# Second block: normalising and turning x by token tile instead of by feature tile

## The chip, the cores and the metric

The kernel runs on one core of a Trainium2 chip. The metric is the device time of one execution in microseconds (us), the lower the better. All tensors are float32. A matmul is made from three float32r passes (low half of one operand times high half of the other, the reverse, and high times high), so each operand exists twice in SBUF: rounded to float32r ("hi") and the rest ("lo").

## The reference

Two transformer blocks run on 512 tokens of width 1024, each with two layers. Only the second block is touched. What matters of it:

```python
def rms_norm(x, g):
    y = x * lax.rsqrt(jnp.mean(x * x, axis=-1, keepdims=True) + EPS)
    return y * g

for l in range(DEPTH):                       # DEPTH = 2
    mod = silu(c) @ w_ada[l] + b_ada[l]      # six vectors of 1024
    sh_m, sc_m, gt_m, sh_f, sc_f, gt_f = jnp.split(mod, 6, axis=-1)
    h = rms_norm(x, g_mix[l]) * (1.0 + sc_m[:, None]) + sh_m[:, None]
    z = h @ w_in[l] + b_in[l]
    ...                                      # two attentions, gates
    x = x + gt_m[:, None] * (merged @ w_out[l])
    h2 = rms_norm(x, g_ffn[l]) * (1.0 + sc_f[:, None]) + sh_f[:, None]
    gate, up = jnp.split(h2 @ w_gu[l], 2, axis=-1)
    x = x + gt_f[:, None] * ((silu(gate) * up) @ w_down[l])
```

## The kernel before

The program is a list of named steps (`steps_second`), and each engine walks the same list in the same order and emits its own part of each step. So the list is the order of the work on every engine; an engine that has to wait in one step does nothing of the steps behind it. Engines meet by semaphores: `bank_full` and `bank_free` for the eight PSUM banks, and one for each kind of result. The second block is a hardware loop over the two layers.

x stands in SBUF with tokens on the partitions, as four token tiles of 128 x 1024 (`x_tok`). The products want features on the partitions. So twice in a layer the normalised x is turned into eight feature tiles of 128 x 512 (`x_pair`): once ahead of the first projection (`which` = 0), once ahead of the gate and up products of the feed-forward part (`which` = 1). These are the steps:

- `rms`, tile tt: ScalarE (ACT) squares x_tok[tt] and sums each row (two instructions: ACTIVATE and READ_ACCUMULATOR). With `which` = 1 it waits for step `add`, in which VectorE (DVE) adds the output of the attention part to that tile: two multiplications from PSUM (L2231) and one addition (L2235).
- `rms_scale`: DVE makes the mean of all four tiles at once (L2075, 128x4), GpSimd (POOL) raises it to the power -0.5 (L2032), and DVE scales the four tiles into `xn` (L2078).
- `turn2`, feature tile d: TensorE (PE) transposes that column of the four xn tiles into one bank (L1821); ACT applies scale and bias of the features and writes the value to SBUF, then copies it, rounded, to `x_pair[0]` (both told as L1917); DVE subtracts the two to get `x_pair[1]` and frees the bank (L2239). The eight d use banks 0, 1, 6, 7 in turn.

The first projection's step `rows qa i` reads feature tiles 2i and 2i+1 and waits for those. The first gate product reads one feature tile after the other and waits for each (`ready`). Weights come through a ring of two slots of 2 MB; SyncE issues a slot's next load once PE has begun to use the other slot. Each piece of weights is rounded by ACT (L642) and its rest made by POOL (L651), at most three pieces ahead in the list; the first four pieces of the first projection come right behind the last `turn2`.

Of the kernel before, what the change touches and what calls it, by code (L numbers as in the profile page):

```python
# [33 lines left out]
F32 = mybir.dt.float32  # L34
# [320 lines left out]
def steps_second():  # L355

    out = []

    def add(name, *args, banks=()):
        out.append((name, args, banks))  # L360

    def rows_of(name):
        add("rows_open", name, banks=(4, 5, 6, 7))
        for i in range(4):
            add("rows", name, i)
        for tt in range(TT):
            add("rows_out", name, tt)
    add("params2")
    add("mod_row", 0, banks=(2,))
    for k in range(4):  # L370
        if k < 3:
            add("mod_row", k + 1, banks=(2 + (k + 1) % 2,))
        add("mod_c", k, banks=(4 + k % 2,))
    def turn_all(which):
        add("rms_scale", which, banks=("power",))
        for d in range(DT):
            add("turn2", which, d, banks=((0, 1, 6, 7)[d % 4],))
    for tt in range(TT):
        add("rms", 0, tt)
    turn_all(0)  # L380
    rows_of("qa")
    add("head_norm", "qa", banks=("power",))
    add("rope", "qa")
    for c in range(4):
        add("rows_T", "qa", c, banks=(2 + c % 2,))
    rows_of("qi")
    add("rope", "qi")
    for c in range(4):
        add("rows_T", "qi", c, banks=(2 + c % 2,))
    rows_of("misc")  # L390
    add("head_norm", "ka", banks=("power",))
    add("rope", "misc")
    for c in range(2):
        add("rows_T", "misc", c, banks=(2 + c % 2,))
    add("open_mask")
    for qt in range(1, TT):
        for h in range(HQ):
            add("idx", qt, h, banks=(h % 2,))
        add("top", qt)

        first = 2 + 2 * qt
        for k in (first, first + 1):
            add("mod_row", k, banks=(2 + k % 2,))
        for k in (first, first + 1):
            add("mod_g" if qt == 1 else "mod_c", k, banks=(4 + k % 2,))

    def attend(a):
        add("s_qk", a, 0, banks=(2,))
        for n in range(TT * HQ + 3):
            if n + 1 < TT * HQ:  # L410
                add("s_qk", a, n + 1, banks=(2 + (n + 1) % 2,))
            if n < TT * HQ:
                add("s_soft", a, n)
            if 2 <= n < TT * HQ + 2:
# [12 lines left out]
            if a == 0 and n in (6, 14):  # L427
                add("mod_g", 10 + n // 8, banks=(1,))
    attend(0)
    for name in ("qb", "kb"):  # L430
        rows_of(name)
        add("head_norm", name, banks=("power",))
        for c in range(4):
            add("rows_T", name, c, banks=(2 + c % 2,))
    rows_of("vb")
    attend(1)
    for n in range(2):
        for dt in range(DT):
            if n or dt > 2:
                add("gate", n, dt, banks=(2 + dt % 2,))  # L440
            if n == 0 and dt in (2, 3, 4, 5):
                add("y2_split", dt - 2)
        for dt in range(DT):
            add("branch", n, dt, banks=(4 + dt % 2,))
            if n == 1 and dt:
                add("merge_split", dt - 1)
    add("merge_split", DT - 1)
    for half in range(2):
        add("out_open", half, banks=tuple(range(4 * half, 4 * half + 4)))
        for i in range(4):  # L450
# [12 lines left out]
    return number(with_splits(out, second_pieces(), {12: ("rows_open", "qb")}))  # L463
# [19 lines left out]
def build(nc, stream, x_in, consts, pack1, ln_rows, edge1, pack2, edge2, pos, c_in, out):  # L483
# [174 lines left out]
    def feed_product(pe, feed, p, out_, begin, right, col=0, ready=None):  # L658

        pe.wait_ge(split_lo, p + 1)  # L660
        release = begin(feed.unit(p))
        w = feed.weights(p)
        k = w[0].shape[1]
        for t in range(k):
            if ready:
                ready(t)
# [990 lines left out]
    rel2 = region(13104, HQ)  # L1657
    stage = region(17200, TT)
    stage_sq = region(19248, TT)
    xn = [region(17200, TT, D), region(7184, TT, D)]  # L1660
    prob2 = region(17200, 4)
    prob2T = region(19248, 2)
    y_rows = region(20272, 2)
# [94 lines left out]
    def second_tensor(pe, layer, steps, uses):  # L1758
# [23 lines left out]
        for name, *args in [(s_[0],) + s_[1] for s_ in steps]:  # L1782
# [30 lines left out]
                        ins = mm(bank[b][:, cols_], C("pick"), sums[:, cols_], True, True)  # L1813
                        ins.then_inc((weights_used, bank_full[b])[half], 1)
            elif name == "turn2":
                which, d = args
                take(b, n)
                for tt in range(TT):
                    if d == 0:
                        pe.wait_ge(xn_ready, which * TT + tt + 1)  # L1820
                    ins = nc.tensor.transpose(bank[b][:, tt * P:(tt + 1) * P], xn[which][:, tt, d * P:(d + 1) * P], C("ident"))  # L1821
                ins.then_inc(bank_full[b], 1)
            elif name in ("rows_open", "out_open"):
                for b, n in zip(banks, use):
                    take(b, n)
            elif name == "rows":
                proj, i = args
                if proj == "qa":
                    for d in (2 * i, 2 * i + 1):
                        drained(pe, uses, "turn2", 0, d)  # L1830
                feed_rows(pe, feed2, feed2.at[name, proj, i], i, uses[("rows_open", proj)][0], x_pair, begin)
            elif name == "rows_T":
                proj, c = args
# [72 lines left out]
                feed_rows(pe, feed2, feed2.at[name, half, i], i, uses[("out_open", half)][0], merged2_pair, begin)  # L1906
            elif name == "gu":
                i, part = args
                take(b, n)
                turned = (lambda t: drained(pe, uses, "turn2", 1, t)) if (i, part) == (0, 0) else None  # L1910
                feed_product(pe, feed2, feed2.at[name, i, part], bank[b][:, :], begin, x_pair, ready=turned).then_inc(bank_full[b], 1)
            elif name in ("down_open", "down", "down_last"):
                feed_down(pe, feed2, name, args[0] if args else None, uses, begin)

    def second_scalar(act, layer, steps, uses):
# [3 lines left out]
        for name, *args in [(s_[0],) + s_[1] for s_ in steps]:  # L1919
# [20 lines left out]
                    .then_inc(square_done, 1)  # L1940
                act.wait_ge(square_done, which * TT + tt + 1)
            elif name == "turn2":
                which, d = args
                if d == 0:
                    act.wait_ge(mod_ready, which + 1)
                filled()
                f(x_lo_value[:, d, :], bank[b][:, :], ACT.Identity, bias=mod[:, 16 * which + d:16 * which + d + 1],
                  scale=gain[:, 8 * which + d:8 * which + d + 1]).then_inc(act_step, 1)
                act.wait_ge(act_step, DT * which + d + 1)
                f(x_pair[0][:, d, :], x_lo_value[:, d, :], ACT.Copy).then_inc(turned_hi, 1)  # L1950
# [70 lines left out]
    def second_gpsimd(pool, layer, steps, uses):  # L2021
        width = {"qa": 32, "ka": 4, "qb": 32, "kb": 32}
        for name, *args in [(s_[0],) + s_[1] for s_ in steps]:
# [3 lines left out]
            if "power" not in banks:  # L2027
                continue
            n = use[banks.index("power")]
            cell = power[:, 0:TT if name == "rms_scale" else width[args[0]]]  # L2030
            pool.wait_ge(stats_ready, n + 1)
            nc.gpsimd.tensor_tensor(cell, cell, half_minus.to_broadcast([P, cell.shape[1]]), ALU.pow).then_inc(power_ready, 1)  # L2032

    def second_vector(dve, layer, steps, uses):
# [6 lines left out]
        for name, *args in [(s_[0],) + s_[1] for s_ in steps]:  # L2041
# [24 lines left out]
            elif name == "mod_g":  # L2066
# [5 lines left out]
            elif name == "rms_scale":  # L2072
                which = args[0]
                dve.wait_ge(square_done, (which + 1) * TT)
                V.tensor_scalar(power[:, 0:TT], sq_sum[:, 0:TT], 1.0 / D, EPS2, ALU.mult, ALU.add).then_inc(stats_ready, 1)  # L2075
                dve.wait_ge(power_ready, uses[(name, which)][1][0] + 1)
                for tt in range(TT):
                    V.tensor_scalar(xn[which][:, tt, :], x_tok[:, tt, :], power[:, tt:tt + 1], None, ALU.mult).then_inc(xn_ready, 1)  # L2078
            elif name == "rows_out":
                proj, tt = args  # L2080
                col, width = ROWS[proj]
# [152 lines left out]
                xs = x_tok[:, tt, :]  # L2234
                V.tensor_tensor(xs, xs, add_tmp[which], ALU.add).then_inc(x_added, 1)  # L2235
            elif name == "turn2":
                which, d = args
                dve.wait_ge(turned_hi, DT * which + d + 1)
                V.tensor_tensor(x_pair[1][:, d, :], x_lo_value[:, d, :], x_pair[0][:, d, :].bitcast(F32), ALU.subtract)\  # L2239
                    .then_inc(bank_free[b], 1)  # L2240
# [244 lines left out]
```

## Time and profile before

| | us |
|---|---|
| median of 3 runs (lowest, highest) | 4796.42 (4795.56, 4799.74) |
| the profiled execution: its time | 4796.42 |
| the profiled execution: its span | 4794.6 |
| PE busy in the span | 4067.4 (85%) |
| DVE, ACT, POOL busy | 1383.3, 1421.9, 1423.7 (29%, 30%, 30%) |

PE is busy most of the time, and each of the others less than a third. The second block begins at 2641 us of the span, and its second layer near 3720 us. The stretches around the two normalisations lie at 2690 to 2715 us and 3317 to 3339 us in layer 0, and again at 3761 to 3786 us and 4389 to 4411 us in layer 1, with the same times inside each to about 0.05 us. A row of a timeline gives start, duration, engine, line, operation, output and inputs, shape, and in brackets how long the engine had been idle and what ended that.

### The profile page before, as it was taken

To read this page: it belongs to the slowest core of one execution; us is meant where nothing else is said; L and a number is where in the kernel's file an instruction comes from. 1 tells how busy PE (TensorE), PEld (TensorE's weight loads), DVE (VectorE), ACT (ScalarE), POOL (GpSimd) and SP (SyncE) were. 2 spreads that over 40 slices of the span, in tenths; PEclk is the share of its full clock that TensorE was granted. 3 is DMA by queue.
4 is the path that set the end of the run, shared out by engine and by line. 5 is a ranking of instruction groups with operands and counts; after the bars stand their busy time and mean duration, and the time that the engine had idled before them with its cause. 6 is when DMAs were issued, how large, how long until landed. Compare 5 with 4: busy or idle time off the path is not lost.

```text
span 4794.6 us, 67666 instructions
## 1 busy us (share of the span) xinstructions
PE 4067.4 (85%) x28944; PEld 3202.7 (67%) x28944; DVE 1383.3 (29%) x2684; ACT 1421.9 (30%) x2380; POOL 1423.7 (30%) x605
## 2 busy tenths in 40 slices
PE   2898889999968979898999477799999467899998
PEld 2688568777856866686877245577887345677886
DVE  2444341311134433413112154213111163213111
ACT  1344242222223431522222213233222213333222
POOL 3200224444440012245444201233443201233443
PEclk9899899999988998998999678899999678899999
DMA  2000212222220001122221332111223231111222
GB/s 86 34 3 3 84 46 99 77 97 88 103 79 7 3 38 68 57 93 79 90 103 71 127 125 87 53 70 71 95 99 114 107 141 65 53 71 71 105 88 106
DMA packets 26699, 366.39 MB, mean 76 GB/s; under 512 B 3104, under 2 KB 3104, under 8 KB 4128
## 3 DMA queue, kind: packets, MB, share of 16 engines
q1 hardware_dynamic: 23040, 335.55, 18.9%
q10 hardware_dynamic: 3360, 26.47, 1.5%
q8 instruction: 235, 3.85, 0.3%
q14 instruction: 64, 0.52, 0.0%
HBM read 359.91 MB, written 2.10 MB: 76 GB/s over the span
## 4 chain that ended last, share of the span: by engine, by line
PE 78%; DVE 11%; ACT 3%; POOL 3%; DMA 2%; issue 2%; DVEq 0%; POOLq 0%; ACTq 0%; PEldq 0%; SPq 0%; PEld 0%
PE bank L581 20%; PE bank L582 20%; PE bank L583 20%; PE bank L854 10%; PE bank L1762 4%; DMA ring<-stream 1%; DVE arena L2173 1%; DVE arena L2172 1%; ACT arena L1165 1%; ACT arena L1917 1%; PE bank L1865 1%; DVE arena L1573 1%; POOL small L2032 1%; PE bank L1794 1%; DVE arena L1476 1%
## 5 line engine op out<-in xcount | busy, mean ns | idle before, releaser
L651 POOL TENSOR_TENSOR ring_r<-ring,hi_ring 128x1024 fp32r<-128x1024 f32 (+1 forms) x522 | 1252.5, 2402 | 2901.9 <-ACT hi_ring L642 2901.5
L581 PE MATMUL bank<-xT_r,ring_r 128*128 128x512 f32 x2288 | 913.7, 399 | 52.3 <-POOL ring_r L651 49.2
L582 PE MATMUL bank<-x_lo_r,hi_ring 128*128 128x512 f32 x2288 | 906.2, 396 | 0.0
L583 PE MATMUL bank<-xT_r,hi_ring 128*128 128x512 f32 x2288 | 902.2, 394 | 0.0
L642 ACT ACTIVATE hi_ring<-ring 128x1024 fp32r<-128x1024 f32 (+1 forms) x522 | 543.9, 1046 | 741.1 <-PE bank L583 391.0
L581 PEld LDWEIGHTS bank<-xT_r,ring_r 128*128 128x128 f32 x2288 | 436.3, 191 | 159.5 <-issue 60.9
L583 PEld LDWEIGHTS bank<-xT_r,hi_ring 128*128 128x128 f32 x2288 | 433.9, 190 | 101.4
L582 PEld LDWEIGHTS bank<-x_lo_r,hi_ring 128*128 128x128 f32 x2288 | 435.4, 190 | 96.5 <-issue 2.1
L854 PE MATMUL bank<-arena 64*64 64x64 f32 (+4 forms) x7456 | 395.3, 250 | 78.3 <-DVE arena L1476 29.6
L1165 ACT ACTIVATE arena<-bank 128x512 f32<-128x512 f32 (+1 forms) x422 | 231.0, 549 | 703.3 <-PE bank L583 496.8
L854 PEld LDWEIGHTS bank<-arena 64*64 64x64 f32 (+2 forms) x7456 | 306.1, 140 | 134.4 <-issue 91.0
L581 PE MATMUL bank<-hi_ring,pairs 128*128 128x512 f32 x864 | 344.3, 399 | 7.6 <-DVE pairs L656 7.6
L582 PE MATMUL bank<-ring_r,pairs 128*128 128x512 f32 x864 | 342.3, 396 | 0.0
L583 PE MATMUL bank<-hi_ring,pairs 128*128 128x512 f32 x864 | 341.9, 396 | 0.0
L1917 ACT ACTIVATE arena<-bank 128x512 f32<-128x512 f32 (+3 forms) x288 | 144.1, 506 | 629.4 <-PE bank L583 190.7
L1762 PE MATMUL bank<-arena 128*128 128x64 f32 (+4 forms) x992 | 232.8, 383 | 85.0 <-DVE small L2196 46.5
L1762 PEld LDWEIGHTS bank<-arena 64*128 64x128 f32 (+1 forms) x992 | 143.7, 207 | 124.0 <-ACT arena L1917 55.2
L656 DVE TENSOR_TENSOR pairs<-arena,pairs 128x512 fp32r<-128x512 f32 x108 | 81.3, 762 | 443.9 <-ACT pairs L647 443.9
L581 PEld LDWEIGHTS bank<-hi_ring,pairs 128*128 128x128 f32 x864 | 164.0, 190 | 48.5 <-issue 9.2
L581 PE MATMUL bank<-hi_ring,x_lo_r 128*128 128x512 f32 (+1 forms) x448 | 175.2, 391 | 22.9 <-POOL ring_r L651 22.9
L1165 ACT ACTIVATE arena<-bank,small 128x64 f32<-128x64 f32 (+1 forms) x222 | 108.9, 496 | 278.8 <-PE bank L583 162.6
L583 PEld LDWEIGHTS bank<-hi_ring,pairs 128*128 128x128 f32 x864 | 163.5, 189 | 39.0
(244 smaller groups left out, 4945.0 us busy)
## 6 DMA issues: line engine op xcount, KB each, us to landing
ring<-stream SPq DMA_DIRECT2D x160, 2048.0 KB, 7.7
arena<-pack ACTq DMA_DIRECT2D x2, 2564.0 KB, 10.3
arena<-ln_rows ACTq DMA_DIRECT2D x5, 1024.0 KB, 5.4
arena<-edge ACTq DMA_DIRECT2D x2, 2048.0 KB, 8.0
arena<-edge ACTq DMA_DIRECT2D x2, 1792.0 KB, 6.8
arena<-pack ACTq DMA_DIRECT2D x2, 1200.5 KB, 5.9
x<-x_in ACTq DMA_DIRECT2D x1, 2048.0 KB, 20.6
out<-x ACTq DMA_DIRECT2D x1, 2048.0 KB, 6.6
```

Source lines behind the costliest of these rows:

```text
L581: first = nc.tensor.matmul(out_, left[1], right[0], start=start, stop=False)
L582: nc.tensor.matmul(out_, left[0], right[1], start=False, stop=False)
L583: return first, nc.tensor.matmul(out_, left[0], right[0], start=False, stop=stop)
L642: nc.scalar.activation(feed.hi(n), feed.raw(n), ACT.Copy).then_inc(split_hi, 1)
L651: nc.gpsimd.tensor_tensor(feed.raw(n, ring_r), feed.raw(n), feed.hi(n).bitcast(F32), ALU.subtract).then_inc(split_lo, 1)
L656: nc.vector.tensor_tensor(lo, feed.hid[:, n, :], hi.bitcast(F32), ALU.subtract).then_inc(hid_lo, 1)
L854: return nc.tensor.matmul(out_, lhsT, rhs, start=start, stop=stop)
L1165: return nc.scalar.activation(out_, in_, func, **kw)
L1476: V.tensor_tensor(T1[g % 2], bank[b][:, :].rearrange("p (b t) -> p b t", b=8), mask.unsqueeze(1).to_broadcast([P, 8, CH]), ALU.mult).then_ ...
L1573: V.tensor_tensor_reduce(out=prob[i % 4][:, m, :], in0=bank[banks[m]][:, :], in1=rel[:, h, at_:at_ + S], scale=1.0, scalar=-3.0e38, op0=AL ...
L1762: return nc.tensor.matmul(out_, lhsT, rhs, start=start, stop=stop)
L1917: return nc.scalar.activation(out_, in_, func, **kw)
```

## The change

`rms_scale` and the turning by feature tile go. Each token tile is taken through by itself: `rms` of tile tt now has its own mean, power (128x1) and scaling, and `turn2` of tile tt transposes the eight 128 x 128 squares of that tile into banks 0 and 1, four to a bank. ACT then applies scale and bias with four instructions of 128 x 128 for each bank (each square has its own features), and copies, and DVE subtracts, four squares at once. `xn` has two tiles instead of four, so scaling tile tt waits until tile tt-2 is turned. With `which` = 0 the steps alternate (`rms` 0, `turn2` 0, `rms` 1, ...); with `which` = 1 `turn2` of a tile comes one tile later. The first projection and the first gate product wait for the last token tile. Squares, transposes, scalings, copies and subtractions have the same number of elements in all; the scale-and-bias instructions become 32 instead of 8 in each turning.

```diff
-    def turn_all(which):
-        add("rms_scale", which, banks=("power",))
-        for d in range(DT):
-            add("turn2", which, d, banks=((0, 1, 6, 7)[d % 4],))
     for tt in range(TT):
-        add("rms", 0, tt)
-    turn_all(0)
+        add("rms", 0, tt, banks=("power",))
+        add("turn2", 0, tt, banks=(0, 1))
...
     for tt in range(TT):
         add("add", 0, tt)
-        add("rms", 1, tt)
-    turn_all(1)
+        add("rms", 1, tt, banks=("power",))
+        if tt:
+            add("turn2", 1, tt - 1, banks=(0, 1))
+    add("turn2", 1, 3, banks=(0, 1))
...
# TensorE
+                which, tt = args
+                pe.wait_ge(xn_ready, which * TT + tt + 1)
+                for i in range(2):
+                    take(banks[i], use[i])
+                    for k in range(4):
+                        ins = nc.tensor.transpose(bank[banks[i]][:, k * P:(k + 1) * P], xn[which][:, tt % 2, (4 * i + k) * P:(4 * i + k + 1) * P],
+                                                  C("ident"))
+                    ins.then_inc(bank_full[banks[i]], 1)
...
-                    for d in (2 * i, 2 * i + 1):
-                        drained(pe, uses, "turn2", 0, d)
+                if proj == "qa" and i == 0:
+                    drained(pe, uses, "turn2", 0, TT - 1)
...
+                if i == 0 and part == 0:
+                    drained(pe, uses, "turn2", 1, TT - 1)
...
# ScalarE
+                for i in range(2):
+                    filled(banks[i], use[i])
+                    for k in range(4):
+                        d = 4 * i + k
+                        ins = f(dst[:, d, tt * P:(tt + 1) * P], bank[banks[i]][:, k * P:(k + 1) * P], ACT.Identity,
+                                bias=mod[:, 16 * which + d:16 * which + d + 1], scale=gain[:, 8 * which + d:8 * which + d + 1])
+                    here = slice(4 * i, 4 * i + 4), slice(tt * P, (tt + 1) * P)
+                    ins.then_inc(act_step, 1)
+                    act.wait_ge(act_step, 8 * which + 2 * tt + i + 1)
+                    f(x_pair[0][:, here[0], here[1]], dst[:, here[0], here[1]], ACT.Copy).then_inc(turned_hi, 1)
...
# VectorE
+            elif name == "rms":
+                dve.wait_ge(square_done, which * TT + tt + 1)
+                V.tensor_scalar(power[:, tt:tt + 1], sq_sum[:, tt:tt + 1], 1.0 / D, EPS2, ALU.mult, ALU.add).then_inc(stats_ready, 1)
+                dve.wait_ge(power_ready, n + 1)
+                if tt >= 2:
+                    drained(dve, uses, "turn2", which, tt - 2)
+                V.tensor_scalar(xn[which][:, tt % 2, :], x_tok[:, tt, :], power[:, tt:tt + 1], None, ALU.mult).then_inc(xn_ready, 1)
```

What ScalarE does ahead of the first projection, before. Rows with `x 128x1024` are the squares, `arena<-bank,small` the scale and bias from PSUM, `xT_r<-arena` the rounded copy; a row says what it waits for, and ends with how many follow each other alike.

```order
L1917 ACTIVATE arena,small<-x 128x1024
L1917 ACTIVATE arena,small<-x 128x1024 [waits square_done] x3
L1917 ACTIVATE arena<-bank,small 128x512 [waits bank0_full,mod_ready,square_done]
L1917 ACTIVATE xT_r<-arena 128x512 [waits act_step]
L1917 ACTIVATE arena<-bank,small 128x512 [waits bank1_full]
L1917 ACTIVATE xT_r<-arena 128x512 [waits act_step]
```

The same place now:

```order
L1914 ACTIVATE arena,small<-x 128x1024
L1914 ACTIVATE arena<-bank,small 128x128 [waits bank0_full,mod_ready,square_done]
L1914 ACTIVATE arena<-bank,small 128x128 x3
L1914 ACTIVATE xT_r<-arena 128x4x128 [waits act_step]
L1914 ACTIVATE arena<-bank,small 128x128 [waits bank1_full]
L1914 ACTIVATE arena<-bank,small 128x128 x3
L1914 ACTIVATE xT_r<-arena 128x4x128 [waits act_step]
L1914 ACTIVATE arena,small<-x 128x1024
```

The four squares stood together ahead of everything; now the square of the second tile stands behind the whole turning of the first.

VectorE between the output product and the gate product, before (L2231 and L2235 are step `add`, L2075 the mean, L2078 the scaling into xn, L2239 the subtraction):

```order
L2231 TENSOR_TENSOR arena<-bank,arena 128x512 [waits bank3_full,x_added]
L2231 TENSOR_TENSOR arena<-bank,arena 128x512 [waits bank7_full,bank3_free]
L2235 TENSOR_TENSOR x<-x,arena 128x1024 [waits bank7_free]
L2075 TENSOR_SCALAR small<-small 128x4 [waits square_done]
L2078 TENSOR_SCALAR arena<-x,small 128x1024 [waits power_ready]
L2078 TENSOR_SCALAR arena<-x,small 128x1024 x3
L2239 TENSOR_TENSOR x_lo_r<-arena,xT_r 128x512 [waits turned_hi] x8
```

The third and fourth tile at that place now (L2235, L2239, L2078, L2082 and L2245 are these steps in the changed file):

```order
L2235 TENSOR_TENSOR arena<-bank,arena 128x512 [waits bank2_full,x_added]
L2235 TENSOR_TENSOR arena<-bank,arena 128x512 [waits bank6_full,bank2_free]
L2239 TENSOR_TENSOR x<-x,arena 128x1024 [waits bank6_free]
L2078 TENSOR_SCALAR small<-small 128x1 [waits square_done]
L2082 TENSOR_SCALAR arena<-x,small 128x1024 [waits bank1_free,bank0_free,power_ready]
L2245 TENSOR_TENSOR x_lo_r<-arena,xT_r 128x4x128 [waits turned_hi] x2
L2235 TENSOR_TENSOR arena<-bank,arena 128x512 [waits bank3_full,x_added]
```

The additions of the four tiles stood ahead of the mean; now mean, scaling and the two subtractions of the tile before stand between one tile's addition and the next one's.

## Rows read from the trace of the kernel before

**Rows 1.** The chain that ended last, by engine, from the page.

```profile
PE 78%; DVE 11%; ACT 3%; POOL 3%; DMA 2%; issue 2%; DVEq 0%; POOLq 0%; ACTq 0%; PEldq 0%; SPq 0%; PEld 0%
```

**Rows 2.** Timeline, layer 0, ahead of the first projection: start, duration, engine, what.

```profile
2690.83 1.05 ACT L1917 ACTIVATE arena<-x 128x1024 f32<-128x1024 f32 x1
...
2694.30 0.17 DVE L2064 TENSOR_TENSOR small<-small,arena 128x8 f32<-128x8 f32 x1
2694.36 1.06 ACT L1917 ACTIVATE arena<-x 128x1024 f32<-128x1024 f32 x1
...
2695.55 0.17 DVE L2075 TENSOR_SCALAR small<-small 128x4 f32<-128x4 f32 x1 [1.07 <-ACT arena L1917]
2695.79 1.02 POOL L2032 TENSOR_TENSOR small<-small 128x4 f32<-128x4 f32 x1 [56.70 <-DVE small L2075]
2696.85 2.74 DVE L2078 TENSOR_SCALAR arena<-x,small 128x1024 f32<-128x1024 f32 x4 [1.14 <-POOL small L2032]
...
2697.66 0.47 PE L1821 MATMUL bank<-const,arena 128*128 128x128 f32 x1 [3.87 <-DVE arena L2078]
...
2699.65 3.93 PE L1821 MATMUL bank<-const,arena 128*128 128x128 f32 x17 [0.19 <-DVE arena L2078]
2700.24 0.78 ACT L1917 ACTIVATE arena<-bank,small 128x512 f32<-128x512 f32 x1 [4.73 <-PE bank L1821]
2701.05 0.63 ACT L1917 ACTIVATE xT_r<-arena 128x512 fp32r<-128x512 f32 x1
2701.59 0.76 ACT L1917 ACTIVATE arena<-bank,small 128x512 f32<-128x512 f32 x1
2701.72 0.69 DVE L2239 TENSOR_TENSOR x_lo_r<-arena,xT_r 128x512 fp32r<-128x512 f32 x1 [2.12 <-ACT xT_r L1917]
...
2710.90 3.88 ACT L642 ACTIVATE hi_ring<-ring 128x1024 fp32r<-128x1024 f32 x4
...
2714.60 0.79 PE L581 MATMUL bank<-hi_ring,x_lo_r 128*128 128x512 f32 x1 [7.03 <-POOL ring_r L651]
```

**Rows 3.** Timeline, layer 0, between the output product and the gate product.

```profile
3317.77 1.06 ACT L1917 ACTIVATE arena<-x 128x1024 f32<-128x1024 f32 x1 [3.59 <-DVE x L2235]
3317.77 1.42 DVE L2231 TENSOR_TENSOR arena<-bank,arena 128x512 f32<-128x512 f32 x2
...
3320.55 1.06 ACT L1917 ACTIVATE arena<-x 128x1024 f32<-128x1024 f32 x1 [1.62 <-DVE x L2235]
...
3325.96 1.06 ACT L1917 ACTIVATE arena<-x 128x1024 f32<-128x1024 f32 x1 [1.55 <-DVE x L2235]
...
3328.43 2.74 DVE L2078 TENSOR_SCALAR arena<-x,small 128x1024 f32<-128x1024 f32 x4 [1.12 <-POOL small L2032]
...
3338.80 0.77 PE L581 MATMUL bank<-xT_r,ring_r 128*128 128x512 f32 x1
```

**Rows 4.** Groups by line and form: busy us, mean ns of one, idle before.

```profile
L1150 ACT ACTIVATE xT_r<-bank 128x512 fp32r<-128x512 f32 x40 | 23.5, 597 | 166.1 <-PE bank L1136 166.1
...
L2078 DVE TENSOR_SCALAR arena<-x,small 128x1024 f32<-128x1024 f32 x16 | 11.0, 749 | 4.5 <-POOL small L2032 4.5
```

**Rows 5.** Timeline of ScalarE in the first block: instructions back to back.

```profile
256.14 1.69 ACT L1165 ACTIVATE arena<-bank,small 128x512 f32<-128x512 f32 x3 [2.24 <-PE bank L854]
...
684.82 0.28 ACT L1165 ACTIVATE arena<-bank 128x128 f32<-128x128 f32 x1 [0.30 <-PE bank L854]
685.00 0.19 ACT L1165 ACTIVATION_READ_ACCUMULATOR arena<-bank 128x1 f32 x1
```

**Rows 6.** Timeline of POOL in the first block: a power of 128x1.

```profile
2607.83 0.55 POOL L1337 TENSOR_TENSOR small<-small 128x1 f32<-128x1 f32 x1 [4.47 <-DVE small L1627]
```

**Rows 7.** Busy time by stretch, layer 0: per engine, then PE clock.

```profile
2714.60:2718.90 4.30, 4.30 (x10) 3.43 (x11) 0.00 (x0) 0.18 (x1) 4.30 (x2) 0.50 0.00 0
2718.90:2723.00 4.10, 4.10 (x19) 3.26 (x19) 0.00 (x0) 0.52 (x1) 2.48 (x2) 0.99 0.00 0
3338.80:3340.20 1.40, 1.40 (x5) 1.14 (x4) 0.77 (x2) 1.37 (x3) 0.00 (x0) 0.50 0.00 0
```

**Rows 8.** Timeline of ScalarE in the projections of layer 0.

```profile
2770.33 0.54 ACT L642 ACTIVATE hi_ring<-ring 128x400 fp32r<-128x400 f32 x1 [8.28 <-DMA ring<-stream]
```

More of the change, by code:

```diff
@@ L656, in feed_vector, with feed_product @@
         nc.vector.tensor_tensor(lo, feed.hid[:, n, :], hi.bitcast(F32), ALU.subtract).then_inc(hid_lo, 1)
-    def feed_product(pe, feed, p, out_, begin, right, col=0, ready=None):
+    def feed_product(pe, feed, p, out_, begin, right, col=0):
         pe.wait_ge(split_lo, p + 1)
@@ L664, in feed_product @@
         for t in range(k):
-            if ready:
-                ready(t)
             first, last = pair_product(out_, [a[:, t, col:col + P] for a in w], [a[:, t, :] for a in right],
@@ L1659, in build @@
     stage_sq = region(19248, TT)
-    xn = [region(17200, TT, D), region(7184, TT, D)]
+    xn = [region(17200, 2, D), region(7184, 2, D)]
     prob2 = region(17200, 4)
@@ L1815, in second_tensor @@
             elif name == "turn2":
[L1816 to L1822, printed above, removed]
+                which, tt = args
[6 more added lines that the diff above has]
+                    ins.then_inc(bank_full[banks[i]], 1)
             elif name in ("rows_open", "out_open"):
@@ L1908, in second_tensor @@
                 i, part = args
+                if i == 0 and part == 0:
+                    drained(pe, uses, "turn2", 1, TT - 1)
                 take(b, n)
-                turned = (lambda t: drained(pe, uses, "turn2", 1, t)) if (i, part) == (0, 0) else None
-                feed_product(pe, feed2, feed2.at[name, i, part], bank[b][:, :], begin, x_pair, ready=turned).then_inc(bank_full[b], 1)
+                feed_product(pe, feed2, feed2.at[name, i, part], bank[b][:, :], begin, x_pair).then_inc(bank_full[b], 1)
             elif name in ("down_open", "down", "down_last"):
@@ L1942, in second_scalar @@
             elif name == "turn2":
-                which, d = args
-                if d == 0:
+                which, tt = args
+                if tt == 0:
                     act.wait_ge(mod_ready, which + 1)
[L1946 to L1950, printed above, removed]
+                dst = x_lo_value
+                for i in range(2):
[8 more added lines that the diff above has]
+                    f(x_pair[0][:, here[0], here[1]], dst[:, here[0], here[1]], ACT.Copy).then_inc(turned_hi, 1)
             elif name in ("split", "hid_split"):
@@ L2029, in second_gpsimd @@
             n = use[banks.index("power")]
-            cell = power[:, 0:TT if name == "rms_scale" else width[args[0]]]
+            cell = power[:, args[1]:args[1] + 1] if name == "rms" else power[:, 0:width[args[0]]]
             pool.wait_ge(stats_ready, n + 1)
@@ L2071, in second_vector @@
                 V.tensor_tensor(o, o, bank[b][:, :], ALU.add).then_inc(bank_free[b], 1)
[L2072 to L2078, printed above, removed]
+            elif name == "rms":
+                which, tt = args
+                dve.wait_ge(square_done, which * TT + tt + 1)
[4 more added lines that the diff above has]
+                V.tensor_scalar(xn[which][:, tt % 2, :], x_tok[:, tt, :], power[:, tt:tt + 1], None, ALU.mult).then_inc(xn_ready, 1)
             elif name == "rows_out":
@@ L2236, in second_vector @@
             elif name == "turn2":
[L2237 to L2240, printed above, removed]
+                which, tt = args
+                for i in range(2):
+                    dve.wait_ge(turned_hi, 8 * which + 2 * tt + i + 1)
+                    here = slice(4 * i, 4 * i + 4), slice(tt * P, (tt + 1) * P)
+                    V.tensor_tensor(x_pair[1][:, here[0], here[1]], x_lo_value[:, here[0], here[1]],
+                                    x_pair[0][:, here[0], here[1]].bitcast(F32), ALU.subtract).then_inc(bank_free[banks[i]], 1)
             elif name == "s_turn" and args[0] == 1:
```

1 line of the change is left out of this document (removed).

## The prediction

> **What bounds the kernel now.** I read the chain that ended last first: 78% of it is PE, 11% DVE, 3% each ACT and POOL [rows 1]. So PE sets the time wherever it has work, and a change of other engines' work counts only where PE stands waiting for it. Then I read the two stretches that the change touches, in the timeline, each in layer 0; layer 1 repeats them.
>
> Ahead of the first projection PE is idle for its next product from the modulation vectors on, except for the transposes. What ends last there is a single file: four squares on ACT from 2690.83 us, the mean, the power, the scalings, and then ACT's eight pairs of scale-and-bias and copy, 1.33 us apart, up to 2710.90 us, where ACT turns to the weights. POOL makes their rest and PE begins at 2714.60 us [rows 2]. The end of ACT's turning sets that start; 3.70 us of weight work follow it.
>
> Ahead of the gate product the additions of x come first, one tile every 2.71 to 2.78 us on DVE, the last square at 3325.96 us; the scalings start at 3328.43 us and PE's first gate product at 3338.80 us [rows 3]. From there PE runs on while the last feature tiles are still being turned, because that product takes them one by one. So the number to compare is 3338.80 us with the moment at which the last token tile is ready after the change.
>
> **The change, part by part.** First, the costs of one tile in the new form. The square to the start of the mean is 1.19 us (2694.36 to 2695.55 us), and from a square to ACT's next instruction 1.18 us (the three intervals from 2690.83 to 2694.36 us) [rows 2]. Mean to power is 0.24 us, then the power, then 0.04 us [rows 2]. The power of 128x4 took 1.02 us there; one of 128x1 took 0.55 us [rows 6]. I take 0.55, together 0.83 us; the other end is 1.02. The scaling is 0.75 us [rows 4], and 0.06 us later PE begins (2697.66 after 2696.85 + 0.75 us) [rows 2]. Four transposes into a bank: the seventeen in 3.93 us are 0.22 us apart, and from the last one of a bank to ACT it is 0.59 us (2699.65 to 2700.24 us), so 3 x 0.22 + 0.59 = 1.25 us [rows 2]. These rows are at half clock (0.50), as PE's are whenever it has been idle here [rows 7]. The second bank's transposes hide behind the first bank's ACT work.
>
> The scale-and-bias on 128x128 isn't in the trace. On 128x512 it takes 0.76 us [rows 2]. A plain one takes 0.60 us at 512 columns [rows 4] and 0.28 us at 128 [rows 5], so I size one at 0.76 - 0.32 = 0.44 us. Back to back they overlap. From below: the plain 128x128 is followed by the next instruction after 0.18 us [rows 5]. From above: no overlap at all, 0.44 us. Between: three of 128x512 with a scale operand took 1.69 us, which is 0.50 us apart for 0.69 us each, an overlap of 0.19 us [rows 5]. That is the nearest row in kind of operand, and I take 0.44 - 0.19, about 0.24 us apart. One bank's share is then 3 x 0.24 + 0.44 + 0.03 = 1.19 us to the copy, and 0.54 us from the copy to ACT's next instruction (2701.05 to 2701.59 us) [rows 2]: 1.73 us, for a tile 3.46 us. A copy of four squares costs what one of 512 columns does, as the first block's copy of that shape shows (0.60 us) [rows 4]. From a copy to DVE's subtraction it is 0.67 us, and that takes 0.69 us [rows 2].
>
> The Trainium skill (ScalarE: Activation LUTs, "What ACT_TABLE_LOAD costs") gives an ACTIVATE a fixed part of 186 ns, about 93 ns more for each per-partition operand, and an overlap of only about 93 ns. Its figures put a 128x128 with both operands at some 0.48 us, spaced 0.39 us: an estimate that would add about 11 us to the sum below. The three instructions above came out closer than that rule has them, 0.50 us apart where it gives 0.61, so I stay with the row [rows 5].
>
> First place. What is late now is no longer ACT's copying alone: the order puts square tt+1 behind turning tt on ACT, and its mean behind it on DVE. Nothing of tile tt+1 overlaps with tile tt. Tile 0: DVE is free after the modulation at about 2694.50 us [rows 2], so the mean starts there, the scaling at 2695.33, the transposes at 2696.14, ACT at 2697.39, done at 2700.85 us. Each further tile is the whole ring: 1.19 + 0.83 + 0.75 + 0.06 + 1.25 + 3.46 = 7.54 us, three of them 22.62 us. ACT turns to the weights at 2723.47 instead of 2710.90 us: 12.57 us later, and PE with it. The finer wait of the projection for two feature tiles hid nothing before, since the weights were later anyway; replacing it costs nothing.
>
> Second place. Tile 0 is added as before; its square starts at 3317.77 us [rows 3]. Then DVE waits: mean at 3318.96, scaling from 3319.79 to 3320.54 us. Only now comes the addition of tile 1, which had started at 3317.77 us. An addition up to the next square is 2.78 us (3317.77 to 3320.55 us) [rows 3], so square 1 is at 3323.32, and ACT starts turning tile 0 at 3324.50 us. Its second subtraction ends 1.73 + 1.19 + 0.67 + 0.69 = 4.28 us later, at 3328.78 us, and lets the addition of tile 2 begin. This ring (addition 2.78, square 1.18, turning 4.28) is 8.24 us, and the scaling of the next tile falls into it beside ACT. Two of them bring the end of turning tile 2 to 3345.26 us. For tile 3 the banks are free only now: 0.06 + 1.25 to the last half's ACT work, 1.19 + 0.67 + 0.69 + 0.05 to PE: 3349.17 us against 3338.80, 10.37 us. The gate product had started with all but its last feature tiles ready; that overlap goes, and is inside this number.
>
> Clock. The gate product ran at half clock (1.2 GHz) for its first 1.40 us, having the transposes close ahead of it; the first projection, after 7.03 us of idle PE, for 4.30 us, before it went to 2.4 GHz [rows 2, 7]. After the change the gate product also follows sparse transposes and about 2.5 us of nothing, so I give it 4.30 us: (4.30 - 1.40) / 2 = 1.45 us more. Below: nothing.
>
> The adds that wait have only the steps of this normalisation behind them; no weight load is queued there. SyncE's loads wait for PE's progress and move with it. After both places the work is PE's again, without slack.
>
> Sum: 2 layers x (12.57 + 10.37 + 1.45) = 48.8 us. The profiled execution took 4796.42 us for a span of 4794.6 us, which is also the median, so the forecast is 4845 us, 1.0% slower. Bounds: spacing of 0.18 us takes 0.18 us from each half, of 0.44 adds 0.60; eight halves are on the path at the first place and seven at the second, 30 in all: -5.4 or +18.0 us. The power at 1.02 us counts at each tile at the first place and once at the second: 2 x 5 x 0.47 = +4.7 us. Clock -2.9 us. So 4837 to 4868 us.
>
> **Rivals.** A, the small ACT instructions don't overlap: the upper end, 4845 + 18 = 4863 us. For it: a scale-and-bias is longer than a plain one, and how two such operands overlap no row shows. Against it: the three back to back [rows 5].
>
> B, the tiles do overlap and it gets faster. The mechanism would be at the second place: the additions keep their pace, and only the last tile remains behind the last square at 3325.96 us [rows 3]. Then 1.19 + 0.83 + 0.75 + 0.06 + 1.25 + 1.73 + 1.19 + 0.67 + 0.69 + 0.05 = 8.41 us lead to 3334.37 us, 4.43 us sooner, and spread transposes keep the clock up, 0.70 us more. At the first place ACT alone would be the bound, 2697.39 + 8 x 1.73 = 2711.23 us, 0.33 us later. In all 2 x (4.43 + 0.70 - 0.33) = 9.6 us gained, 4787 us, and 4783 with the tighter spacing. It decides from the point where DVE's addition of tile 1 starts before the scaling of tile 0. Against it: DVE and ACT take the list in order, and the wait stands ahead of the addition.
>
> C, part of the delay is hidden by a transfer that would have been waited for anyway: ACT stood 8.28 us for weights after the second projection had begun [rows 8]. If those came at a fixed time, 2 x 8.3 us would be given back: 4829 us. Against it: that load is issued only when PE takes the slot before it.
>
> D, both places are covered by something I don't see, and the time stays.
>
> **How the numbers follow.** Forecast 0.79, A 0.12, C 0.03, B 0.04, D 0.02. The range of 4828 to 4868 us takes in the forecast's bounds, A and C, with some 1 in 10 outside. What a measurement of this kernel can tell from no change is about 0.2%, 9.6 us. Slower: forecast, A and C, 0.94. B lies at that edge, so faster 0.03 and within 0.2% 0.03.
>
> **What would show it.** Right: at the first place squares on ACT about 7.5 us apart, with ACT and DVE idle in between for PE; at the second place additions about 8.2 us apart where they were 2.7; PE's idle time ahead of the first gate product up by some 10 us; DVE's waits for ACT's copies grown. The spacing of four 128x128 on ACT gives the disputed price directly. Wrong: squares of four tiles close together, a gate product starting less than 25 us after the first square of its place, or a stage between the two places that has become shorter.

## The result, and the profile after

The changed kernel takes 4853.55 us in the median (4852.16 to 4857.79, 4 runs), the kernel before in the same runs 4795.99 us (4792.81 to 4799.74, 4 runs). The ratio is 1.0118 with a 95% interval of 1.0103 to 1.0134: 57.6 us, or 1.2%, slower. Forecast were 48.8 us and 4845 us, with a range of 4828 to 4868 us. Of all executions told below one, of the kernel with the small instructions alone, took 13941 us; it counts in the median of its six and stands outside the ratio.

First the changed kernel's page, busy time by engine and the chain that ended last:

```profile
PE 4068.8 (84%) x28944; PEld 3207.1 (66%) x28944; DVE 1387.2 (29%) x2696; ACT 1445.4 (30%) x2476; POOL 1428.4 (29%) x617
...
PE 77%; DVE 11%; ACT 4%; POOL 3%; issue 3%; DMA 2%; DVEq 0%; POOLq 0%; ACTq 0%; PEldq 0%; SPq 0%; PEld 0%
```

PE does the work that it did (4068.8 us busy against 4067.4), and the span grew by 55.6 us. So most of the time went into waits of PE, and a little into its clock, shown below. ACT is 23.5 us busier, on 96 more instructions; in the chain ACT went from 3% to 4% and "issue" from 2% to 3% [rows 1].

The first place in layer 0, from the end of the modulation to the first weight piece, two tiles of the four, and then PE's first product (timeline: start, duration, engine, what):

```profile
2690.91 0.17 DVE L2067 TENSOR_TENSOR small<-small,arena 128x8 f32<-128x8 f32 x1
2691.00 0.15 DVE L2078 TENSOR_SCALAR small<-small 128x1 f32<-128x1 f32 x1
2691.22 0.55 POOL L2035 TENSOR_TENSOR small<-small 128x1 f32<-128x1 f32 x1 [55.42 <-DVE small L2078]
2691.81 0.75 DVE L2082 TENSOR_SCALAR arena<-x,small 128x1024 f32<-128x1024 f32 x1 [0.66 <-POOL small L2035]
...
2692.62 1.97 PE L1817 MATMUL bank<-const,arena 128*128 128x128 f32 x8 [2.22 <-DVE arena L2082]
2693.85 1.50 ACT L1914 ACTIVATE arena<-bank,small 128x128 f32<-128x128 f32 x4 [5.27 <-PE bank L1817]
2695.39 0.63 ACT L1914 ACTIVATE xT_r<-arena 128x512 fp32r<-128x512 f32 x1
2695.92 1.49 ACT L1914 ACTIVATE arena<-bank,small 128x128 f32<-128x128 f32 x4
...
2697.44 0.63 ACT L1914 ACTIVATE xT_r<-arena 128x512 fp32r<-128x512 f32 x1
2697.98 1.04 ACT L1914 ACTIVATE arena<-x 128x1024 f32<-128x1024 f32 x1
...
2706.11 1.04 ACT L1914 ACTIVATE arena<-x 128x1024 f32<-128x1024 f32 x1
...
2722.38 3.88 ACT L640 ACTIVATE hi_ring<-ring 128x1024 fp32r<-128x1024 f32 x4
...
2726.08 0.79 PE L579 MATMUL bank<-hi_ring,x_lo_r 128*128 128x512 f32 x1 [7.07 <-POOL ring_r L649]
```

This answers to [rows 2]. The square of each next tile (`x 128x1024`) comes right behind the copy of the tile before, and the squares are 8.13 us apart (2697.98, 2706.11 us): the single file. From the end of the modulation to the weights it is now 2722.38 - 2690.91 = 31.47 us, and was 2710.90 - 2694.30 = 16.60 us: 14.87 us more in this layer, where 12.57 were forecast. PE's product begins 3.70 us behind that in both kernels.

The second place in layer 0, ACT's squares and DVE's additions, then PE's first gate product:

```profile
3331.47 1.06 ACT L1914 ACTIVATE arena<-x 128x1024 f32<-128x1024 f32 x1 [3.59 <-DVE x L2239]
...
3332.66 0.15 DVE L2078 TENSOR_SCALAR small<-small 128x1 f32<-128x1 f32 x1 [1.22 <-ACT arena L1914]
3333.48 0.75 DVE L2082 TENSOR_SCALAR arena<-x,small 128x1024 f32<-128x1024 f32 x1 [0.67 <-POOL small L2035]
3334.15 1.41 DVE L2235 TENSOR_TENSOR arena<-bank,arena 128x512 f32<-128x512 f32 x2
...
3342.35 0.69 DVE L2245 TENSOR_TENSOR x_lo_r<-arena,xT_r 128x512 fp32r<-128x512 f32 x1 [1.36 <-ACT xT_r L1914]
3342.96 1.41 DVE L2235 TENSOR_TENSOR arena<-bank,arena 128x512 f32<-128x512 f32 x2
...
3351.70 1.41 DVE L2235 TENSOR_TENSOR arena<-bank,arena 128x512 f32<-128x512 f32 x2
...
3364.89 0.79 PE L579 MATMUL bank<-xT_r,ring_r 128*128 128x512 f32 x1 [3.19 <-issue]
```

The additions (L2235 here) start at 3334.15, 3342.96 and 3351.70 us, 8.8 us apart where they were 2.7 [rows 3], each right behind the scaling or the last subtraction of a tile. From the first square to the gate product it is 33.42 us, before 21.03 us: 12.39 us more, forecast 10.37.

Busy time by stretch of the changed kernel around the start of the gate product (start and end, its length, then busy us and instructions of PE, its weight loads, DVE, ACT and POOL; the number behind POOL's is PE's clock):

```profile
3364.89:3371.00 6.11, 6.11 (x14) 4.78 (x15) 0.00 (x0) 0.03 (x1) 2.37 (x1) 0.50 0.69 244
3371.10:3375.00 3.90, 3.90 (x19) 3.16 (x18) 0.69 (x1) 1.47 (x2) 0.00 (x0) 1.00 0.35 147
```

It runs at half clock (1.2 GHz) for 6.1 us, where it was 1.4 us before and 4.3 us had been forecast [rows 7]. Half of the 4.7 us more is 2.35 us, forecast 1.45. The first projection went the other way. Its product begins at half clock in both kernels, but for a shorter time in the changed one:

```profile
2726.08:2729.20 3.12, 3.12 (x7) 2.48 (x8) 0.00 (x0) 0.18 (x1) 3.12 (x2) 0.50 0.02 5
3827.91:3831.80 3.89, 3.89 (x9) 3.12 (x10) 0.00 (x0) 0.18 (x1) 3.89 (x2) 0.50 0.00 0
```

These are its layers 0 and 1. The kernel before had about 4.4 us in layer 0 and 5.3 us in layer 1, here the latter:

```profile
3785.55:3790.80 5.25, 5.25 (x12) 4.12 (x13) 0.00 (x0) 0.18 (x1) 5.25 (x3) 0.50 0.00 0
```

That is 1.3 us less in each layer now, which gives back 0.65 us a layer. Together 2 x (14.87 + 12.39 + 2.35 - 0.65) = 57.9 us; the medians differ by 57.6 us. The spans of the two profiles differ by 55.6 us only, because the part ahead of the first place, which the change doesn't touch, was 3.4 us shorter in this one (2690.91 against 2694.30 us at the same instruction). In the profiles of the next five kernels that instruction lies between 2688.36 and 2695.54 us, so the span of a single profile tells a change to some us and no better.

### The profile page after: what moved, and what is told of

Same layout as the page of the kernel before. It is cut to its first block, busy times and chain, and to the rows that moved or that the text cites. A ratio compares the mean times of both kernels' runs of the same rounds, so it can differ in the third digit from the quotient of the medians.

```text
span 4850.2 us, 67804 instructions
## 1 busy us (share of the span) xinstructions
PE 4068.8 (84%) x28944; PEld 3207.1 (66%) x28944; DVE 1387.2 (29%) x2696; ACT 1445.4 (30%) x2476; POOL 1428.4 (29%) x617
## 4 chain that ended last, share of the span: by engine, by line
PE 77%; DVE 11%; ACT 4%; POOL 3%; issue 3%; DMA 2%; DVEq 0%; POOLq 0%; ACTq 0%; PEldq 0%; SPq 0%; PEld 0%
PE bank L579 20%; PE bank L580 20%; PE bank L581 19%; PE bank L850 10%; PE bank L1758 4%; ACT arena L1914 2%; DVE arena L2177 1%; DVE arena L2176 1%; ACT arena L1161 1%; PE bank L1861 1%; DMA ring<-stream 1%; DVE arena L1569 1%; POOL small L2035 1%; PE bank L1790 1%; DVE arena L1472 1%
```

## The experiments

Two theories. O: the order of the list puts the tiles in single file, and an engine's wait for one tile holds up its work on the next. P: the price of splitting eight scale-and-bias instructions into thirty-two is what costs, whatever the order. All kernels were timed against the kernel before on the same chip.

**The new form at one place only.** Both kernels hold both forms. The first has the new one ahead of the first projection:

```diff
     for tt in range(TT):
-        add("rms", 0, tt)
-    turn_all(0)
+        add("rms_t", 0, tt, banks=("power",))
+        add("turn_t", 0, tt, banks=(0, 1))
```

> The kernel before with the new form at the first place only (ahead of the first projection); the turning ahead of the gate product stays by feature tile. Theory O (the order of the list puts the tiles in single file, and each place pays by itself): the first place costs what it costs in the changed kernel, 14.9 us a layer from the first square to ACT's first weight piece, and the second nothing: 2 x 14.9 = 30 us, 4826 us. Theory P (the price of the small ScalarE instructions is all of it, the same at both places): 8 halves x 0.74 us = 5.9 us a layer, 4808 us.

Measured: 4826.17 us, ratio 1.0061 (1.0048 to 1.0074). From the first square to the weights it was 34.95 us, 14.88 more than before; the second place took 21.02 us, as before. The second has it ahead of the gate product:

```diff
-        add("rms", 1, tt)
-    turn_all(1)
+        add("rms_t", 1, tt, banks=("power",))
+        if tt:
+            add("turn_t", 1, tt - 1, banks=(0, 1))
+    add("turn_t", 1, 3, banks=(0, 1))
```

> The kernel before with the new form at the second place only (ahead of the gate product). Theory O: 12.4 us a layer until the gate product starts and about 2 us more for its longer stretch at half clock, 2 x 14.5 = 29 us, 4825 us; together with the first place this makes the whole change. Theory P: about 12 us in all, 4808 us.

Measured: 4823.38 us, ratio 1.0057 (1.0045 to 1.0070). PE's first gate product in its timeline:

```profile
3350.06 0.79 PE L583 MATMUL bank<-xT_r,ring_r 128*128 128x512 f32 x1 [3.33 <-DVE x_lo_r L2282]
```

The first square of that place was at 3316.51 us, so this is 33.55 us behind it, as in the changed kernel. The two places cost 30 and 28 us. Together that is 58 us against 57.6, closer than the intervals promise, since each ratio is known to about 6 us. So within that they add up, and neither is given back later. P's numbers for them (12 us each) are far off.

**The small instructions alone.** The kernel before with the scale-and-bias split, everything else as it was:

```diff
-                f(x_lo_value[:, d, :], bank[b][:, :], ACT.Identity, bias=mod[:, 16 * which + d:16 * which + d + 1],
-                  scale=gain[:, 8 * which + d:8 * which + d + 1]).then_inc(act_step, 1)
+                for k in range(4):
+                    ins = f(x_lo_value[:, d, k * P:(k + 1) * P], bank[b][:, k * P:(k + 1) * P], ACT.Identity,
+                            bias=mod[:, 16 * which + d:16 * which + d + 1], scale=gain[:, 8 * which + d:8 * which + d + 1])
+                ins.then_inc(act_step, 1)
```

> The kernel before, turned by feature tile, but with each scale-and-bias of 128x512 done as four of 128x128 (the price of the small instructions alone, with the order as it was). Theory P: this alone gives most of the 57 us of the change. Theory O: a pair of ACT steps grows from 1.33 to 2.07 us, 8 x 0.74 = 5.9 us a layer at the first place; at the second the gate product's last feature tile becomes ready about 4.8 us later than PE wants it; 2 x (5.9 + 4.8) = 21 us, 4817 us.

Measured: 4817.57 us, ratio 1.0043 (1.0030 to 1.0056), 22 us. At the first place, from the first square to the weights, 25.89 us, 5.82 more than before, as O had it. At the second the total was right and its parts not: the gate product began 23.93 us after the first square, 2.9 us later than before, because the transposes wait for banks that ACT empties more slowly; and then it ran at half clock for 5.3 us instead of 1.4:

```profile
3350.05:3355.40 5.35, 5.35 (x15) 4.18 (x14) 2.08 (x3) 5.29 (x14) 0.00 (x0) 0.50 0.67 214
3355.40:3360.00 4.60, 4.60 (x21) 3.49 (x20) 1.38 (x3) 3.75 (x6) 2.23 (x1) 1.00 0.49 210
```

2.9 + 1.9 = 4.8 us; none of it was the expected wait for the last feature tile, since PE ran without a gap from 3350.05 us on. So the price of the small instructions is real, but it is 22 us with the old order, not 57.

**The order.** The changed kernel, all tiles normalised before the first is turned. That needs four xn tiles in place of two, so the wait for tile tt-2 goes too, and the scratch of the squares lies elsewhere (the diff below shows the order only). In the changed kernel's trace the two xn tiles held nothing up at these places: each scaling in layer 0 started 0.66 or 0.67 us after DVE fell idle, and its power (POOL) ended that.

```diff
-        add("rms", 0, tt, banks=("power",))
-        add("turn2", 0, tt, banks=(0, 1))
+        add("rms", 0, tt, banks=("power",))
+    for tt in range(TT):
+        add("turn2", 0, tt, banks=(0, 1))
...
         add("add", 0, tt)
-        add("rms", 1, tt, banks=("power",))
-        if tt:
-            add("turn2", 1, tt - 1, banks=(0, 1))
-    add("turn2", 1, 3, banks=(0, 1))
+    for tt in range(TT):
+        add("rms", 1, tt, banks=("power",))
+    for tt in range(TT):
+        add("turn2", 1, tt, banks=(0, 1))
```

> The changed kernel with its small instructions and turning by token tile, but ordered so that all four tiles are added and normalised before the first is turned (xn has four tiles again, and the scratch of the squares lies elsewhere for that). Theory O: most of the loss goes. First place: ACT turns from 2697.4 us (by the times of the kernel before) for 4 x 4.14 us, 3 us a layer later than before instead of 14.9. Second place: the gate product starts 7.4 us later instead of 12.4, its half clock stays: 2 x (3 + 7.4 + 2) = 25 us, 4821 us. Theory P: no change from the changed kernel, 4853 us.

Measured: 4818.24 us, ratio 1.0048 (1.0035 to 1.0061). ACT at the first place (timeline):

```profile
2684.89 1.05 ACT L1915 ACTIVATE arena<-x 128x1024 f32<-128x1024 f32 x1
...
2700.48 1.51 ACT L1915 ACTIVATE arena<-bank,small 128x128 f32<-128x128 f32 x4
2702.02 0.63 ACT L1915 ACTIVATE xT_r<-arena 128x512 fp32r<-128x512 f32 x1
...
2708.78 3.88 ACT L641 ACTIVATE hi_ring<-ring 128x1024 fp32r<-128x1024 f32 x4
```

23.89 us from the first square to the weights, 3.8 more than before, against 14.9 in the changed kernel. The same small instructions run here with hardly a gap. At the second place the gate product began 29.36 us after the first square (3315.41 to 3344.77 us), 8.3 more than before. The half clock did not stay as expected; it was half as long as in the changed kernel:

```profile
3344.77:3347.90 3.13, 3.13 (x7) 2.47 (x8) 0.00 (x0) 0.03 (x1) 2.37 (x1) 0.50 0.50 99
```

This kernel and the one before it have the same ScalarE instructions in two good orders and cost about the same, 22 and 23 us. Of the change's 57.6 us some 35 therefore go with the order and 22 with the instructions, by these two differences, each known to about 6 us.

**One step moved.** The changed kernel with the next tile's addition ahead of this tile's scaling:

```diff
+    add("add", 0, 0)
     for tt in range(TT):
-        add("add", 0, tt)
+        if tt + 1 < TT:
+            add("add", 0, tt + 1)
         add("rms", 1, tt, banks=("power",))
```

> The changed kernel with one line of the list moved: at the second place the addition of tile tt+1 stands ahead of the mean and scaling of tile tt. The same instructions. Theory O (DVE's wait for square and power stands ahead of the next addition, and ACT's turning behind it): the gate product starts about 7.3 us a layer sooner than in the changed kernel, 4839 us. Rival (the ACT work of the turning is the bound at this place): no change, 4853 us.

Measured: 4837.01 us, ratio 1.0090 (1.0074 to 1.0105). DVE at the second place:

```profile
3328.85 1.42 DVE L2237 TENSOR_TENSOR arena<-bank,arena 128x512 f32<-128x512 f32 x2
3330.30 1.22 DVE L2241 TENSOR_TENSOR x<-x,arena 128x1024 f32<-128x1024 f32 x1
3331.44 0.15 DVE L2080 TENSOR_SCALAR small<-small 128x1 f32<-128x1 f32 x1
3332.26 0.75 DVE L2084 TENSOR_SCALAR arena<-x,small 128x1024 f32<-128x1024 f32 x1 [0.67 <-POOL small L2037]
3332.93 1.41 DVE L2237 TENSOR_TENSOR arena<-bank,arena 128x512 f32<-128x512 f32 x2
```

The mean (L2080) now starts without a wait for its square, which ran beside the addition, and the third addition comes 4.1 us after the second instead of 8.8. The gate product began 25.52 us after the first square, 7.9 us sooner than in the changed kernel. No instruction was added or taken away, so this is the place of the wait in the list, with what follows from it (the half clock behind it was 3.6 us long instead of 6.1).

**A better version, in three steps.** Since the first place is a single file before the change too, its squares, mean, power and scalings can go where the engines idle, ahead of the modulation vectors (the kernel before, turning by feature tile kept):

```diff
     add("params2")
+    for tt in range(TT):
+        add("rms", 0, tt)
+    add("rms_scale", 0, banks=("power",))
     add("mod_row", 0, banks=(2,))
```

> The kernel before with squares, mean, power and scaling of the first place moved ahead of the modulation vectors, where ACT, DVE and POOL are idle and x is ready. Turning by feature tile stays. If those steps are the single file that the rows of before show there, ACT starts turning when the modulation is ready (2694.5 us instead of 2700.24 us): 5.7 us a layer, 11 us in all, 4785 us. Rival (PE's start hangs on the weights, loaded from 2691 us on): less, down to nothing.

Measured: 4786.01 us, ratio 0.9981 (0.9972 to 0.9990). PE's product began 14.91 us after the modulation was ready (2693.98 to 2708.89 us), before 20.30 us: 5.4 us a layer, 10.8 in all; the medians differ by 8.8 us, known to some 4 us. The next step puts the first weight pieces among the turning:

```diff
+        at_ = at[early[p]] if p in early else max(floor, first[max(p - AHEAD, 0)])
...
+                              {p: ("turn2", 0, p + 3) for p in range(4)}))
```

> As the one before, and the first four weight pieces of the first projection are split among the turning of feature tiles 3 to 6 instead of behind tile 7. PE could then start when piece 0 and feature tiles 0 and 1 are ready: by the load that is issued at 2691 us near 2702 us instead of 2714.6 us: 12 us a layer, 24 us in all, 4772 us. Rival (PE then waits for the later feature tiles, or DVE's subtractions and POOL's splits slow each other): some 15 us in all, 4781 us.

Measured: 4792.47 us, ratio 0.9993 (0.9984 to 1.0002): neither of the two forecasts, and most of the gain of the step before was lost. In its timeline:

```profile
2702.74 10.62 POOL L655 TENSOR_TENSOR ring_r<-ring,hi_ring 128x1024 fp32r<-128x1024 f32 x4 [38.01 <-ACT hi_ring L646]
...
2706.30 2.10 DVE L2243 TENSOR_TENSOR x_lo_r<-arena,xT_r 128x512 fp32r<-128x512 f32 x1 [0.67 <-ACT xT_r L1921]
2708.57 5.93 DVE L2243 TENSOR_TENSOR x_lo_r<-arena,xT_r 128x512 fp32r<-128x512 f32 x3 [0.17 <-ACT xT_r L1921]
...
2714.91 0.79 PE L585 MATMUL bank<-hi_ring,x_lo_r 128*128 128x512 f32 x1 [8.11 <-DVE x_lo_r L2243]
```

POOL's splits ran from 2702.74 us and the first took 2.34 us, so the first piece was ready by 2705.1 us, but PE stood 8.11 us for a subtraction, and began 18.70 us after the modulation (20.28 us in layer 1, as before). DVE's subtractions had taken 0.69 us each [rows 2]. The last row above merges three of unlike length; asked one by one, with a narrow window for each, they are:

```profile
2708.57 2.58 DVE L2243 TENSOR_TENSOR x_lo_r<-arena,xT_r 128x512 fp32r<-128x512 f32 x1 [0.17 <-ACT xT_r L1921]
2711.07 2.83 DVE L2243 TENSOR_TENSOR x_lo_r<-arena,xT_r 128x512 fp32r<-128x512 f32 x1
2713.83 0.68 DVE L2243 TENSOR_TENSOR x_lo_r<-arena,xT_r 128x512 fp32r<-128x512 f32 x1
```

So the four that ran beside POOL's splits took 1.61, 2.10, 2.58 and 2.83 us, and the last, behind them, 0.68 again. The products' own step opens banks 4 to 7, and feature tiles 6 and 7 had used banks 6 and 7: PE could not start before the very last subtraction, which the slow ones ahead of it had put off. So the turning got other banks:

```diff
-            add("turn2", which, d, banks=((0, 1, 6, 7)[d % 4],))
+            add("turn2", which, d, banks=(((0, 1, 2, 3), (0, 1, 6, 7))[which][d % 4],))
```

> As the one before (normalising ahead of the modulation, weight pieces split among the turning), and the turning ahead of the first projection uses banks 0, 1, 2, 3 in place of 0, 1, 6, 7. Reason: the last run's PE waited until DVE's last subtraction, which is when the products' own banks 6 and 7 come free, not for its operands. Theory B (the banks held PE back): PE starts when the first weight piece is done, 8 to 11 us a layer sooner, 4772 us. Rival (DVE's subtractions, 2.1 us each beside POOL's splits, hold it back in any case): as before, 4792 us.

Measured: 4771.20 us (4765.75 to 4774.04), ratio 0.9944 (0.9931 to 0.9958), about 25 us faster than the kernel before, and 82 us faster than the changed one.

```profile
2692.51 0.17 DVE L2068 TENSOR_TENSOR small<-small,arena 128x8 f32<-128x8 f32 x1
...
2705.55 6.05 DVE L2243 TENSOR_TENSOR x_lo_r<-arena,xT_r 128x512 fp32r<-128x512 f32 x3 [0.16 <-ACT xT_r L1921]
```

```profile
2702.67 1.12 PE L1825 MATMUL bank<-const,arena 128*128 128x128 f32 x4 [4.08 <-DVE x_lo_r L2243]
2703.43 0.78 PE L585 MATMUL bank<-hi_ring,x_lo_r 128*128 128x512 f32 x1
```

PE begins at 2703.43 us, right behind its transposes and 10.92 us after the modulation (10.33 us in layer 1), while DVE is still subtracting until 2711.6 us, as slowly as before. Only the banks changed: it was through them that the slow subtractions had held PE. Against the kernel before, the two starts come 9.4 and 10.0 us sooner, 19.4 of the 25 us; where the rest lies is not shown.

## Why the prediction was right, and where its sizes were off

**The mechanism.** Right at both places. That ACT's square and DVE's addition stand behind waits of the tile before is shown by the rows of the changed kernel and by the two kernels that only changed the order. Nothing was hidden or given back: rivals B, C and D are out. Rival A's end (4863 us) lies above the measured time, and its premise of no overlap at all is wrong too.

**The spacing of the small ACT instructions.** This is the term that was mis-sized. Forecast 0.24 us between starts, at 0.44 us each. Measured by form in the changed kernel:

```profile
L1914 ACT ACTIVATE arena<-bank,small 128x128 f32<-128x128 f32 x128 | 47.8, 453 | 28.0 <-PE bank L1817 27.8
```

0.453 us each is close. Four take 1.50 us, so they are (1.50 - 0.453) / 3 = 0.35 us apart, an overlap of 0.10 us, not the 0.19 taken. A bank's share is 2.07 us instead of 1.73; with 30 of them on the path this is 10.2 us, about what the sum lacked (8.8 us against the medians, 9.1 us against the profile's terms). The step that failed is the reading of one row of [rows 5]: "128x512 ... x3" in 1.69 us was taken for three of that shape, 0.50 us apart. Grouped by form, that stretch of the kernel before has another shape among them:

```profile
L1165 ACT ACTIVATE arena<-bank,small 128x512 f32<-128x512 f32 x2 | 1.4, 688 | 2.3 <-PE bank L854 2.2
L1165 ACT ACTIVATE arena<-bank,small 128x64 f32<-128x64 f32 x1 | 0.3, 308 | 0.0
```

Asked piece by piece, the second starts 0.80 us after the first, behind a gap, and the third, 128x64, 0.59 us after the second of 0.69 us: an overlap of 0.10 us, the same as in the new form. The Trainium skill's figures (ScalarE: Activation LUTs, "What ACT_TABLE_LOAD costs"), set aside because of that row, gave 0.48 us each and 0.39 us apart; the trace has 0.453 and 0.35, nearer to them than the forecast was. What they would add to the sum was worked out wrong beside it: 3 x 0.15 us for the spacing and 0.04 us for the length are 0.49 us a bank, over thirty about 14 to 15 us, not 11. With it the change would cost some 63 us, an estimate 6 us above the measured 57.6, where the forecast lies 9 us below.

**The ring of a tile.** At the first place forecast 7.54 us, measured 8.13; at the second 8.24 against 8.8. With 2.07 us for a bank's share, 7.54 becomes 8.22 and 8.24 becomes 8.92; the rest of the ring was 0.1 us shorter than its terms. The power of 128x1 took 0.55 us, as its row in the first block had said [rows 6].

**The clock.** At the gate product the direction was right and the size too small: 6.1 us at half clock instead of 4.3. PE had been idle but for eight transposes every 8.8 us. The extra cost is 2.35 us a layer, with 1.45 forecast. At the first projection the forecast took no change, and 0.65 us a layer came back. Nor does layer 1 repeat layer 0 there, as it does elsewhere to 0.05 us: 5.3 against 4.4 us at half clock in the kernel before.

**The finer wait of the first projection.** That it hid nothing was right, but there was a second reason that the prediction missed: the step that opens the products' banks waits for feature tiles 6 and 7 anyway. That decided the last two experiments. The finer wait of the gate product did hide something, and was inside the number for the second place.

## What to carry to other kernels

Where all engines walk one list in order, cutting a stage into tiles overlaps nothing by itself: look at what each engine now waits for ahead of the work of the next tile, and let independent work (here the next addition, the next square) stand ahead of the wait. Work whose inputs are ready belongs ahead of the late input, and a bank that the next stage opens must not be the last one that this stage empties. And before a price is read from a merged row of a timeline, ask for the shapes in it.

## What was not expected of the hardware

DVE's subtraction of 128x512 took 0.69 us alone and 1.6 to 2.9 us while POOL ran its splits of 128x1024 back to back, in both kernels with the early weights. POOL's took 10.62 and 10.73 us for four, 9.35 in the changed kernel. The kernel before has such rows too, in both blocks. In the first row below a subtraction of the same shape, 0.68 us at other times, ran beside a split of POOL (3261.07 to 3263.68 us):

```profile
3261.54 2.68 DVE L2255 TENSOR_TENSOR merged_lo<-arena,merged_hi 128x512 fp32r<-128x512 f32 x1
3314.57 0.69 DVE L2231 TENSOR_TENSOR arena<-bank,arena 128x512 f32<-128x512 f32 x1 [21.64 <-PE bank L583]
3315.30 2.44 DVE L2235 TENSOR_TENSOR x<-x,arena 128x1024 f32<-128x1024 f32 x1
```

The last two both began beside one split (3314.26 to 3316.66 us). The multiplication that reads a PSUM bank kept its 0.69 us; the addition with both inputs in SBUF took 2.44 us where the others took 1.23. No experiment here took that apart. In the last version it cost little: PE ran without a gap from its first product on, but its last transposes had waited for a subtraction of 1.61 us, up to 0.9 us a layer.

What sets how long PE stays at half clock was not tried by itself. It is not simply how empty PE had been: ahead of the first projection the changed kernel's PE had less to do than the kernel before's, and its half clock was shorter (3.2 and 4.0 us against 4.4 and 5.3); at the gate product it had less to do too, and its half clock was longer (6.1 us against 1.4).
